# The order of the weight slots in a gated linear recurrent unit: the first y slot goes ahead of both gate slots

## The chip, the cores and the metric

The kernel runs on one core of one Trainium2 chip. The metric is the device time of one execution, in microseconds. The core's engines work at once and are ordered only by semaphores: TensorE multiplies matrices, ScalarE, VectorE and GpSimd work on elements, and SyncE issues most transfers.

## What is computed

The program is two transformer blocks over 256 tokens of width 1024: a retention mixer, a feed-forward layer, a recurrent unit (RG-LRU), a second feed-forward layer, and then a second block with an RWKV mixer, neighbourhood attention and a PEER layer. The change touches the recurrent unit alone, some 142 us of the 2104:

```
proj = x @ w_in
y_branch, u = jnp.split(proj, 2, axis=-1)          # 1536 columns each
y_branch = jax.nn.gelu(y_branch, approximate=True)
u = causal_conv4(u) + conv_b
gates = sigmoid(blockwise(u) @ gate_w + gate_b)    # 6 blocks of 256, two gates: r, i
log_a = -8 * r * softplus(-a_param)
a = exp(log_a);  b = sqrt(-expm1(2 * log_a)) * (i * u)
h[t] = a[t] * h[t-1] + b[t]                        # along the 256 tokens
return (h * y_branch) @ w_out
```

## The kernel before

**Products.** A float32 product is made of three products in a shorter type: each operand is split in a high part (a copy by ScalarE) and a low part (the difference, by VectorE), and `mm3` multiplies hi·hi, lo·hi and hi·lo.

**Slots.** All weights stream through two buffers of `SLOT` = 4096 elements per partition (2 MB; a gate slot fills 3072 of them). The list of slots is fixed; slot s uses buffer s % 2. For each slot four engines work in turn: SyncE loads it as soon as the low parts of slot s - 2 are made (`s_wlo`); ScalarE's `split_hi` (L1094, its copies are L1104) makes four pieces of the high part, once the slot is there and TensorE has drained slot s - 2 (`s_wused`); VectorE's `split_lo` (L1585) makes four pieces of the low part behind them; TensorE's `weights` (L2371) waits for the last of these.

**The recurrent unit.** Its eight slots are three u, two gate and three y slots, in the order of `LRU_STEPS`; behind them come three slots of `lru_out`, whose products add up over all twelve blocks. `LRU_STEPS` sets the order of SyncE's loads and of TensorE's work. ScalarE's and VectorE's orders are written out by hand, call by call, and must name the slots in the same order. Here a unit n is one pair of 128-wide blocks, n = 0 to 5:

- `padded(n)` (ScalarE) takes the product of a half u slot out of its bank; `convolved(n)` (VectorE, six instructions at L1806) makes the convolution; `input_hi(n)` and `input_lo(n)` split it.
- Gate products of pair n (TensorE, `gate_products`, 24 matmuls) need `input_lo(n)` and two of four banks; pair n uses banks (2n) % 4 and (2n+1) % 4, so pair 2 must wait until `sigmoids(0)` (ScalarE) has emptied those of pair 0, and so on. A gate slot holds three pairs.
- `decays(n..n+2)` (ScalarE: six exponentials L1241, six tanh L1247), `input_scale(n)` (VectorE, three instructions from L1828), `roots` (ScalarE, L1254), GpSimd's product of i and u (L1065), `scanned(n)` (VectorE, L1837 and two scans L1839).
- `gelus(n)` (ScalarE, L1260) takes y slot n out of its two banks; `gated(n)` (VectorE, L1847) multiplies h by it; `hidden_hi(n)`, `hidden_lo(n)` split the product, which slot n // 2 of `lru_out` needs.

The recurrence buffers are four (`LRU_BUFFERS`): `sigmoids(4)` waits for `gated(0)`, `sigmoids(5)` for `gated(1)`. Sigmoid, exponential (with tanh), square root and gelu each need a table of their own in ScalarE, so that a change from one to another costs an ACT_TABLE_LOAD; copies work with any table. The work behind the unit, from the last slot of `lru_out` on, is one chain: squares, `post_norm`, `norm(3)`, transposes, and the second feed-forward layer.

Of the kernel before, what the change touches and what calls it, by code (L numbers as in the profile page):

```python
# [174 lines left out]
SLOTS = {}  # L175
# [3 lines left out]
    SLOTS[_name] = sum(n for _, n in SLOTS.values()), _n  # L179
SLOTS = {k: v[0] for k, v in SLOTS.items()}  # L180

LRU_STEPS = [("u", 0), ("u", 1), ("u", 2), ("gate", 0), ("y", 0), ("gate", 1), ("y", 1), ("y", 2)]
LRU_UNITS = {"u": 2, "y": 2, "gate": 0}
LRU_SIZE = {"u": SLOT, "y": SLOT, "gate": 3072}
LRU_BUFFERS = 4
# [283 lines left out]
def first_and_second_block(nc, A, consts, out, mods, upto=99):  # L469
    cols = lambda name: consts[:, CONST_AT[name][0]:sum(CONST_AT[name])]  # L470
    with ExitStack() as ctx:
# [619 lines left out]
        def _(act):  # L1091
# [126 lines left out]
            def split_step(kind, n):  # L1218
                split_hi(lru_slot(kind, n), **lru_size(kind, n))
# [36 lines left out]
            def gelus(n):  # L1256

                for half in range(2):
                    b = take(lru_unit("y", n, half))
                    nc.scalar.activation(Y[:, 4 * n + 2 * half:4 * n + 2 * half + 2, :],  # L1260
                                         PS[:, b, :].rearrange("p (b t) -> p b t", b=2),
                                         ACT.Gelu_apprx_tanh).then_inc(s_free[b], 1)

            def padded(n):

                i, half = n // 2, n % 2
                b = take(lru_unit("u", i, half))
                if n >= 2:
                    act.wait_ge(s_uc, n - 1)
                src = PS[:, b, :].rearrange("p (b t) -> p b t", b=2)  # L1270
                nc.scalar.activation(UP[:, 2 * half:2 * half + 2, 3:3 + S], src, ACT.Copy)
                for q in range(2):
                    c = 2 * n + q
                    ins = nc.scalar.activation(UC[:, c, :], PS[:, b, half_of(q)], ACT.Identity,
                                               scale=pcol[:, PCW + 36 + c:PCW + 37 + c], bias=pcol[:, PCB + c:PCB + c + 1])
                ins.then_inc(s_free[b], 1)

            def input_hi(n):

                act.wait_ge(s_uc, n + 1)  # L1280
                nc.scalar.activation(UH[:, 2 * n:2 * n + 2, :], UC[:, 2 * n:2 * n + 2, :], ACT.Copy).then_inc(s_uhi, 1)
# [15 lines left out]
            padded(2)  # L1297
            input_hi(2)
            padded(3)
            split_step("gate", 0)  # L1300
            input_hi(3)
            padded(4)
            input_hi(4)
            padded(5)
            split_step("y", 0)
            sigmoids(0)
            input_hi(5)
            sigmoids(1)
            sigmoids(2)
            split_step("gate", 1)  # L1310
            decays(range(3))
            split_step("y", 1)
            roots(range(3))
            gelus(0)
            for n in range(3, 6):
                sigmoids(n)
            split_step("y", 2)
            hidden_hi(0)
            hidden_hi(1)
            decays(range(3, 6))  # L1320
            split_hi(SLOTS["lru_out"])
            roots(range(3, 6))
            gelus(1)
            hidden_hi(2)
# [245 lines left out]
        def _(dve):  # L1570
# [222 lines left out]
            def split_step(kind, n):  # L1793
                split_lo(lru_slot(kind, n), **lru_size(kind, n))
# [63 lines left out]
            input_lo(1)  # L1858
            convolved(2)
            input_lo(2)  # L1860
            split_step("gate", 0)
            convolved(3)
            input_lo(3)
            convolved(4)
            input_lo(4)
            split_step("y", 0)
            convolved(5)
            input_lo(5)
            split_step("gate", 1)
            for n in range(3):  # L1870
                input_scale(n)
            split_step("y", 1)
            for n in range(3):
                scanned(n)
            gated(0)
            gated(1)
            split_step("y", 2)
            hidden_lo(0)
            hidden_lo(1)
            for n in range(3, 6):  # L1880
                input_scale(n)
            split_lo(SLOTS["lru_out"])
            scanned(3)
            gated(2)
            gated(3)
# [1109 lines left out]
```

## Time and profile before

| | |
|---|---|
| median of 3 runs | 2109.35 us (2107.25 to 2112.37) |
| the profiled execution | 2105.89 us, of which the traced span is 2104.1 us |
| mean granted TensorE clock in it | 0.972 |
| TensorE busy | 1926.8 us (92%) |
| VectorE busy | 1413.4 us (67%) |
| ScalarE busy | 1041.1 us (49%) |

The busy shares are means over stages with different limits. The times in the rows below are microseconds from the span's start; the recurrent unit's products run from 469.6 to 577 us, and those of `lru_out` from 577.7 to 611.4 us.

### The profile page before, as it was taken

Reading aid. Unit: us, or ns where it says so; the run is one execution under the profiler, and the core shown is the slowest. Engines: PE = TensorE matmul, PEld = TensorE weight load, DVE = VectorE, ACT = ScalarE, POOL = GpSimd, SP = SyncE. Lnnn points to the kernel's source line nnn. Section 1 sums busy time; section 2 is a strip of 40 time slices with the busy share of each in tenths; the row PEclk is TensorE's granted clock in tenths of the full one; section 3 lists DMA queues with packets and bytes.
Section 4 is the critical chain, followed back from the end, with each engine's and each line's share of the span. In section 5 each row is a group of like instructions: output and inputs, shape, how many; then the busy total and the mean of one; then the engine's idle time right before and its main releaser. Section 6 shows DMA issues by size and latency. Waiting matters only on the chain.

```text
span 2104.1 us, 40562 instructions
## 1 busy us (share of the span) xinstructions
PE 1926.8 (92%) x15311; PEld 1723.1 (82%) x15311; DVE 1413.4 (67%) x2268; ACT 1041.1 (49%) x2078; POOL 391.4 (19%) x330
## 2 busy tenths in 40 slices
PE   6998899978889999998888769999999999999996
PEld 6875788868879888997767669999999997777775
DVE  5545587777766667325544558998899986666665
ACT  4343443445855444333444334545777765555554
POOL 2202000000100000000000003888666760000000
PEclk9999999999999999999999979999999999999998
DMA  7452556664364785413001554565544446655663
GB/s 272 170 191 90 196 186 227 234 219 139 140 220 156 249 298 201 148 71 59 2 3 43 126 122 111 165 181 152 150 141 141 140 133 189 190 189 189 189 189 130
DMA packets 212577, 333.56 MB, mean 159 GB/s; under 512 B 23494, under 2 KB 140860, under 8 KB 212424
## 3 DMA queue, kind: packets, MB, share of 16 engines
q1 hardware_dynamic: 208888, 320.06, 48.0%
q0 software_dynamic: 3536, 11.34, 1.6%
q8 instruction: 111, 1.82, 0.4%
q14 instruction: 42, 0.34, 0.1%
HBM read 330.26 MB, written 1.08 MB: 157 GB/s over the span
## 4 chain that ended last, share of the span: by engine, by line
PE 70%; DVE 15%; issue 4%; ACT 4%; DMA 2%; PEld 2%; SPq 1%; PEldq 0%; DVEq 0%; POOL 0%; ACTq 0%
PE psum L2345 20%; PE psum L2347 19%; PE psum L2346 19%; PE psum L2952 3%; DVE u_turned L2247 3%; DVE weights_lo L1585 2%; PE psum L2787 1%; PE psum L2776 1%; ACT weights_hi L1104 1%; PE psum L2781 1%; PEld psum L2345 1%; PEld psum L2346 1%; PEld psum L2347 1%; DMA rows<-mods_dram 1%; DVE lru_u L1806 1%
## 5 line engine op out<-in xcount | busy, mean ns | idle before, releaser
L1585 DVE TENSOR_TENSOR weights_lo<-weights,weights_hi 128x1024 fp32r<-128x1024 f32 (+2 forms) x336 | 345.5, 1086 | 272.4 <-ACT weights_hi L1104 267.1
L2345 PE MATMUL psum<-input_hi,weights_hi 128*128 128x256 f32 x1288 | 370.9, 288 | 14.2 <-DVE input_lo L1612 5.2
L1104 ACT ACTIVATE weights_hi<-weights 128x1024 fp32r<-128x1024 f32 (+2 forms) x336 | 289.2, 931 | 177.6 <-PEq L2392 118.0
L1083 POOL TENSOR_TENSOR u_lo<-u_turned,u_hi 128x512 fp32r<-128x512 f32 x256 | 330.7, 1314 | 200.5 <-ACT u_hi L1482 200.5
L2346 PE MATMUL psum<-input_lo,weights_hi 128*128 128x256 f32 x1288 | 367.0, 285 | 0.0
L2347 PE MATMUL psum<-input_hi,weights_lo 128*128 128x256 f32 x1288 | 366.8, 285 | 0.0
L2345 PE MATMUL psum<-input_hi,u_hi 128*128 128x256 f32 x1024 | 296.8, 290 | 6.4 <-POOL u_lo L1083 5.4
L2347 PE MATMUL psum<-input_hi,u_lo 128*128 128x256 f32 x1024 | 290.9, 284 | 0.0
L2346 PE MATMUL psum<-input_lo,u_hi 128*128 128x256 f32 x1024 | 290.7, 284 | 0.0
L2345 PEld LDWEIGHTS psum<-input_hi,weights_hi 128*128 128x128 f32 x1288 | 249.7, 194 | 29.5 <-issue 27.7
L2346 PEld LDWEIGHTS psum<-input_lo,weights_hi 128*128 128x128 f32 x1288 | 249.8, 194 | 0.0
L2347 PEld LDWEIGHTS psum<-input_hi,weights_lo 128*128 128x128 f32 x1288 | 249.6, 194 | 0.0
L2345 PE MATMUL psum<-v_hi,act_hi 128*128 128x512 f32 x512 | 203.7, 398 | 0.0
L2345 PEld LDWEIGHTS psum<-input_hi,u_hi 128*128 128x128 f32 x1024 | 197.5, 193 | 7.2 <-issue 5.8
L2347 PE MATMUL psum<-v_hi,act_lo 128*128 128x512 f32 x512 | 200.2, 391 | 0.0
L2346 PE MATMUL psum<-v_lo,act_hi 128*128 128x512 f32 x512 | 199.8, 390 | 0.0
L2346 PEld LDWEIGHTS psum<-input_lo,u_hi 128*128 128x128 f32 x1024 | 197.7, 193 | 0.0
L2347 PEld LDWEIGHTS psum<-input_hi,u_lo 128*128 128x128 f32 x1024 | 197.3, 193 | 0.0
L1482 ACT ACTIVATE u_hi<-u_turned 128x512 fp32r<-128x512 f32 x256 | 146.9, 628 | 0.0
L2319 DVE TENSOR_TENSOR act_lo<-act_table,act_hi 128x256 fp32r<-128x256 f32 x128 | 54.5, 425 | 133.8 <-ACT act_hi L1557 133.8
L1557 ACT ACTIVATE act_hi<-act_table 128x256 fp32r (+1 forms) x128 | 53.5, 418 | 166.5 <-PE psum L2347 166.2
L2247 DVE STREAM_TRANSPOSE u_turned<-u_rows 128x1024 f32<-128x1024 f32 x100 | 122.9, 1231 | 10.6 <-DMA u_rows<-in_peer_u_dram 9.8
(387 smaller groups left out, 3660.9 us busy)
## 6 DMA issues: line engine op xcount, KB each, us to landing
u_rows<-in_peer_u_dram SPq DMA_DIRECT2D x400, 128.0 KB, 2.5
weights<-in_ffn_w_in_dram SPq DMA_DIRECT2D x44, 1024.0 KB, 7.3
v_rows_even<-in_peer_v_dram SPq DMA_DIRECT2D x64, 512.0 KB, 3.5
v_rows_odd<-in_peer_v_dram SPq DMA_DIRECT2D x64, 512.0 KB, 3.4
weights<-in_ret_w_in_dram SPq DMA_DIRECT2D x24, 1024.0 KB, 7.4
ada_rows_in<-in_ada_w_dram SPq DMA_DIRECT2D x24, 1024.0 KB, 5.2
weights<-in_ffn_w_out_dram SPq DMA_DIRECT2D x44, 512.0 KB, 6.5
u_rows_more<-in_peer_u_dram SPq DMA_DIRECT2D x112, 128.0 KB, 2.6
```

What stands on the lines that cost most here:

```text
L1083: nc.gpsimd.tensor_tensor(UTL[:, b, half, :], turned[:, half, :], UTH[:, b, half, :].bitcast(F32), ALU.subtract).then_inc(s_ul[b], 1)
L1104: nc.scalar.activation(whi[:, r, at_], wraw[:, r, at_], ACT.Copy).then_inc(s_whi[r], 1)
L1482: nc.scalar.activation(UTH[:, b, half, :], turned[:, half, :], ACT.Copy).then_inc(s_uh[b], 1)
L1557: nc.scalar.activation(AH[:, j % 2:j % 2 + 1, :], GT[:, bass.ds(4 * i + j, 1), :], ACT.Copy)\
L1585: ins = nc.vector.tensor_tensor(wlo[:, r, at_], wraw[:, r, at_], whi[:, r, at_].bitcast(F32), ALU.subtract)
L1806: chain.done(nc.vector.scalar_tensor_tensor(o, UP[:, 2 * half + q, tap:tap + S], pcol[:, c:c + 1], o, ALU.mult, ALU.add))
L2247: nc.vector.transpose(UT[j % 4].rearrange("p k (c e) -> p c k e", c=4), (UR, UR2)[at_ // 2][:, at_ % 2, :].rearrange("p (c k j) -> p c k j ...
L2319: nc.vector.tensor_tensor(AL[:, b:b + 1, :], GT[:, bass.ds(4 * i + j, 1), :], AH[:, b:b + 1, :].bitcast(F32), ALU.subtract).then_inc(s_as, 1)
L2345: nc.tensor.matmul(o, ah, bh, start=start, stop=False)
L2346: nc.tensor.matmul(o, ah, bl, start=False, stop=False)
L2347: return nc.tensor.matmul(o, al, bh, start=False, stop=stop)
L2952: ins = nc.tensor.matmul(PS[:, 4 + g % 4, x * P:(x + 1) * P], ONE[:, g % 2, 1, x, :], ONE[:, g % 2, 0, x, :], start=True, stop=True)
```

## The change

`LRU_STEPS` goes from u, u, u, gate, y, gate, y, y to u, u, u, y, gate, gate, y, y. SyncE and TensorE follow it by themselves. ScalarE's and VectorE's calls are put in a new order. The instructions are the same, and as many.

```diff
--- before.py
+++ after.py
@@ -179,7 +179,7 @@
     SLOTS[_name] = sum(n for _, n in SLOTS.values()), _n
 SLOTS = {k: v[0] for k, v in SLOTS.items()}
 
-LRU_STEPS = [("u", 0), ("u", 1), ("u", 2), ("gate", 0), ("y", 0), ("gate", 1), ("y", 1), ("y", 2)]
+LRU_STEPS = [("u", 0), ("u", 1), ("u", 2), ("y", 0), ("gate", 0), ("gate", 1), ("y", 1), ("y", 2)]
 LRU_UNITS = {"u": 2, "y": 2, "gate": 0}
 LRU_SIZE = {"u": SLOT, "y": SLOT, "gate": 3072}
 LRU_BUFFERS = 4
@@ -1297,28 +1297,29 @@
             padded(2)
             input_hi(2)
             padded(3)
-            split_step("gate", 0)
+            split_step("y", 0)
             input_hi(3)
             padded(4)
             input_hi(4)
+            split_step("gate", 0)
             padded(5)
-            split_step("y", 0)
+            input_hi(5)
+            split_step("gate", 1)
             sigmoids(0)
-            input_hi(5)
             sigmoids(1)
             sigmoids(2)
-            split_step("gate", 1)
+            split_step("y", 1)
+            sigmoids(3)
+            gelus(0)
+            split_step("y", 2)
             decays(range(3))
-            split_step("y", 1)
             roots(range(3))
-            gelus(0)
-            for n in range(3, 6):
+            split_hi(SLOTS["lru_out"])
+            for n in range(4, 6):
                 sigmoids(n)
-            split_step("y", 2)
             hidden_hi(0)
             hidden_hi(1)
             decays(range(3, 6))
-            split_hi(SLOTS["lru_out"])
             roots(range(3, 6))
             gelus(1)
             hidden_hi(2)
@@ -1858,28 +1859,30 @@
             input_lo(1)
             convolved(2)
             input_lo(2)
-            split_step("gate", 0)
+            split_step("y", 0)
             convolved(3)
             input_lo(3)
             convolved(4)
             input_lo(4)
-            split_step("y", 0)
+            split_step("gate", 0)
             convolved(5)
             input_lo(5)
             split_step("gate", 1)
-            for n in range(3):
-                input_scale(n)
             split_step("y", 1)
-            for n in range(3):
-                scanned(n)
+            input_scale(0)
+            split_step("y", 2)
+            input_scale(1)
+            input_scale(2)
+            scanned(0)
             gated(0)
+            scanned(1)
             gated(1)
-            split_step("y", 2)
+            scanned(2)
+            split_lo(SLOTS["lru_out"])
             hidden_lo(0)
             hidden_lo(1)
             for n in range(3, 6):
                 input_scale(n)
-            split_lo(SLOTS["lru_out"])
             scanned(3)
             gated(2)
             gated(3)
```

ScalarE, from the end of the sixth convolution on, as a difference (`weights_hi` is a slot's high part, 128x768 for a gate slot and 128x1024 for others; `lru_r` and `lru_i` from psum are the sigmoids, `lru_a` the exponentials, `lru_y` the gelus):

```order
 L1231 ACTIVATE lru_i<-psum,param_cols 128x256 x2
 L1104 ACTIVATE weights_hi<-weights 128x1024 x4
+L1231 ACTIVATE lru_r<-psum,param_cols 128x256 x2
+L1231 ACTIVATE lru_i<-psum,param_cols 128x256 x2
+L1260 ACT_TABLE_LOAD
+L1260 ACTIVATE lru_y<-psum 128x512 x2
+L1104 ACTIVATE weights_hi<-weights 128x1024 x4
+L1241 ACT_TABLE_LOAD
+L1241 ACTIVATE lru_a<-lru_r,small 128x256 x6
+L1247 ACTIVATE lru_r<-lru_r,small 128x256 x6
```

The row of L1104 at the top is the high part of the second y slot, which now stands right behind the sigmoids of the first three pairs; the fourth pair's sigmoids, the first gelus and the third y slot's high part follow, and only then the exponentials and tanh of the first three pairs.

VectorE, from the second gate slot's low part on, in the kernel before:

```order
L1585 TENSOR_TENSOR weights_lo<-weights,weights_hi 128x768 x4
L1828 TENSOR_TENSOR lru_q<-lru_a 128x512
L1829 SCALAR_TENSOR_TENSOR lru_r<-lru_q,lru_r 128x512
L1830 TENSOR_SCALAR lru_r<-lru_r 128x512
L1828 TENSOR_TENSOR lru_q<-lru_a 128x512
L1829 SCALAR_TENSOR_TENSOR lru_r<-lru_q,lru_r 128x512
L1830 TENSOR_SCALAR lru_r<-lru_r 128x512
```

and in the kernel of the change (each line number is one higher):

```order
L1586 TENSOR_TENSOR weights_lo<-weights,weights_hi 128x768 x4
L1586 TENSOR_TENSOR weights_lo<-weights,weights_hi 128x1024 x4
L1829 TENSOR_TENSOR lru_q<-lru_a 128x512
L1830 SCALAR_TENSOR_TENSOR lru_r<-lru_q,lru_r 128x512
L1831 TENSOR_SCALAR lru_r<-lru_r 128x512
L1586 TENSOR_TENSOR weights_lo<-weights,weights_hi 128x1024 x4
L1829 TENSOR_TENSOR lru_q<-lru_a 128x512
L1830 SCALAR_TENSOR_TENSOR lru_r<-lru_q,lru_r 128x512
```

The second y slot's low part moved ahead of `input_scale(0)`, and the third y slot's low part stands between `input_scale(0)` and `input_scale(1)`.

## Rows read from the trace of the kernel before

**Rows 1.** Chain of waits, 469 to 590 us: share of the stretch by engine and line.
```profile
by line: DVE weights_lo L1585 20.9%; DVE lru_u L1806 12.8%; issue 10.2%; ACT weights_hi L1104 7.7%; ACT lru_a L1241 4.1%; ACT lru_u L1274 3.9%; DVE lru_r L1839 3.6%; DVE lru_r L1829 3.5%; PE psum L2345 3.4%; DVE lru_i L1837 3.3%; DVE lru_q 
```

**Rows 2.** Timeline, TensorE: start us, duration us, operation, [idle before it <- releaser].
```profile
505.69 0.36 PE L2345 MATMUL psum<-lru_hi,weights_hi 128*128 128x256 f32 x1 [0.37 <-issue]
...
519.60 0.55 PE L2345 MATMUL psum<-lru_hi,weights_hi 128*128 128x256 f32 x1 [7.93 <-ACT lru_r L1231]
...
547.76 0.55 PE L2345 MATMUL psum<-lru_hi,weights_hi 128*128 128x256 f32 x1 [5.35 <-ACT lru_r L1231]
...
577.74 0.47 PE L2345 MATMUL psum<-weights_hi,lru_hi 128*128 128x512 f32 x1 [0.50 <-issue]
...
589.29 0.50 PE L2345 MATMUL psum<-weights_hi,lru_hi 128*128 128x512 f32 x1 [0.40 <-DVE weights_lo L1585]
```

**Rows 3.** Timeline, VectorE, 503 to 590 us.
```profile
503.08 3.08 DVE L1806 SCALAR_TENSOR_TENSOR lru_u<-lru_padded,param_cols,lru_u 128x256 f32<-128x256 f32 x6
...
519.05 3.99 DVE L1806 SCALAR_TENSOR_TENSOR lru_u<-lru_padded,param_cols,lru_u 128x256 f32<-128x256 f32 x6
...
534.27 0.69 DVE L1828 TENSOR_TENSOR lru_q<-lru_a 128x512 f32<-128x512 f32 x1 [2.79 <-ACT lru_r L1247]
...
539.65 4.63 DVE L1585 TENSOR_TENSOR weights_lo<-weights,weights_hi 128x1024 fp32r<-128x1024 f32 x4
...
544.91 1.27 DVE L1839 TENSOR_TENSOR_SCAN lru_r<-lru_a,lru_i 128x256 f32<-128x256 f32 x2
...
551.24 1.42 DVE L1847 TENSOR_TENSOR lru_u<-lru_r,lru_y 128x512 f32<-128x512 f32 x2
...
556.05 4.81 DVE L1585 TENSOR_TENSOR weights_lo<-weights,weights_hi 128x1024 fp32r<-128x1024 f32 x4 [3.39 <-ACT weights_hi L1104]
...
564.48 0.69 DVE L1828 TENSOR_TENSOR lru_q<-lru_a 128x512 f32<-128x512 f32 x1 [2.42 <-ACT lru_r L1247]
...
584.61 4.63 DVE L1585 TENSOR_TENSOR weights_lo<-weights,weights_hi 128x1024 fp32r<-128x1024 f32 x4
```

**Rows 4.** Timeline, ScalarE, 498 to 560 us.
```profile
498.72 3.05 ACT L1104 ACTIVATE weights_hi<-weights 128x768 fp32r<-128x768 f32 x4
...
512.04 0.58 ACT L1271 ACTIVATE lru_padded<-psum 128x512 f32<-128x512 f32 x1
...
513.41 3.89 ACT L1104 ACTIVATE weights_hi<-weights 128x1024 fp32r<-128x1024 f32 x4
...
517.33 1.28 ACT L1231 ACT_TABLE_LOAD   x1
...
518.62 0.84 ACT L1231 ACTIVATE lru_r<-psum,param_cols 128x256 f32<-128x256 f32 x2
...
530.93 2.51 ACT L1241 ACTIVATE lru_a<-lru_r,small 128x256 f32<-128x256 f32 x6
...
544.38 1.08 ACT L1260 ACTIVATE lru_y<-psum 128x512 f32<-128x512 f32 x2
...
558.63 1.20 ACT L1286 ACTIVATE lru_hi<-lru_u 128x512 fp32r<-128x512 f32 x2
```

**Rows 5.** Timeline, GpSimd, 520 us.
```profile
520.27 1.44 POOL L1065 TENSOR_TENSOR lru_i<-lru_i,lru_u 128x512 f32<-128x512 f32 x1 [53.29 <-ACT lru_i L1231]
```

**Rows 6.** Weight slots, 468 to 600 us: DMA issue to landing.
```profile
DMA to landing us min/median/max: 4.5/6.7/9.3
```

**Rows 7.** Windows: window, length, busy time, then PEclk, DMA share, GB/s.
```profile
519.60:524.20 4.60, 4.43 (x24) 4.23 (x24) 3.70 (x6) 1.66 (x5) 1.44 (x1) 0.67 0.82 285
547.70:553.40 5.70, 5.46 (x24) 5.20 (x24) 4.82 (x6) 2.08 (x6) 1.66 (x1) 0.51 0.61 249
```

**Rows 8.** Timeline, TensorE, later in the program.
```profile
1181.63 0.79 PE L2345 MATMUL psum<-weights_hi,input_hi 128*128 128x512 f32 x1 [6.16 <-DVE weights_lo L1585]
...
1349.12 0.56 PE L2345 MATMUL psum<-input_hi,u_hi 128*128 128x256 f32 x1 [2.54 <-POOL u_lo L1083]
...
1431.82 0.36 PE L2345 MATMUL psum<-input_hi,u_hi 128*128 128x256 f32 x1 [2.90 <-POOL u_lo L1083]
```

## Prediction, made before the changed kernel was run

> **What bounds the kernel now.** I read the chain of waits of the recurrent unit first. Its largest shares are VectorE's low parts (20.9%), the convolutions (12.8%) and ScalarE's high parts (7.7%); TensorE's largest line has 3.4% [rows 1]. So in this stage the end is set by ScalarE and VectorE, not by TensorE. TensorE's own timeline says the same: it stands still for 7.93 us in the first gate slot and for 5.35 us in the second, both times until ScalarE's sigmoids empty a bank, and runs slow behind each [rows 2]. What decides the stage, however, is where the two sides meet. The first slot of the output product starts at 577.74, its second at 589.29, 0.40 us after TensorE had nothing left, and the releaser is the low part of that slot's weights [rows 2]. VectorE makes it from 584.61 to 589.24 [rows 3]. TensorE's finish (588.9) and VectorE's finish (589.24) are thus equal within half a microsecond. What makes TensorE earlier gives nothing, and what makes VectorE later costs in full: behind this slot comes one serial chain of products, norm and transposes with no slack to eat a delay.
>
> So I follow VectorE's program. Counted back from 589.24 it has two waits for ScalarE, 3.39 us at 556.05 and 2.42 us at 564.48, and before them one of 2.79 us, ended at 534.27 by the first tanh [rows 3]. From `input_scale(0)` at 534.27 to the low part of the second output slot at 589.24 are 55.0 us. I call the start of `input_scale(0)` S, and ask of the change: when is S, and how long is the tail behind it.
>
> **Up to the gates.** The first y slot takes the first gate slot's place. Its high parts take 3.89 instead of 3.05 us [rows 4]; its low parts take 4.63, and those of a gate slot three quarters of that, 3.5, so the convolutions behind are 1.1 us late. The y slot's low parts are there at 498.7 + 1.1 + 4.6 = 504.4, and TensorE begins it at 505.69 as it now begins the gate slot [rows 2]. The transfers have 6.7 us, at most 9.3, from issue to landing, and each slot's issue comes over 12 us before its high part; I cost the moved loads at nothing [rows 6]. TensorE does 48 matmuls in 511.67 - 505.69 = 6.0 us [rows 2], so the y slot's 96 end at 517.7. Gate 0's high part now stands ahead of `padded(5)`. That one began at 512.04 and took 1.4 [rows 4]; the high part begins at 512.04 + 1.2 = 513.2, its low part ends at 513.2 + 0.9 + 3.5 = 517.6, just in time. `padded(5)` ends at 513.2 + 3.05 + 1.4 = 517.7 and the sixth convolution at 520.8. That is 2.2 us earlier than before (523.04), 0.9 of it because no GpSimd product runs beside it: the same six instructions take 3.08 us alone and 3.99 us beside GpSimd's at 520.27 [rows 3, 5].
>
> **From there to S**, all on ScalarE. `input_hi(5)` 0.6 gives 521.4; gate 1's high part 3.05, 524.5; table load 1.28, 525.8; sigmoids are 0.73 a gate (0.84 for the two less their overlap) [rows 4]. The first bank is free at 526.6. TensorE did its 48 gate matmuls from 517.8 to 523.8, so it waits 2.8 us instead of 7.93. Here a first unknown: pair 2's 24 matmuls take 2.9 us at full clock, and took 4.43 us at 0.67 and 5.46 us at 0.51 granted after the two waits of now [rows 7]. Later in the program one wait of 2.54 us was followed by a slow matmul (0.56 us for the first) and one of 2.90 by a fast one (0.36) [rows 8]. So I keep both: pair 2 ends at 529.5 or 531.1, its sigmoids at 530.5 or 532.0. Then the second y slot's high part 3.9 (534.4 or 535.9), `sigmoids(3)` 1.5 (535.9 or 537.4), table load and two gelus 2.4 (538.3 or 539.8) [rows 4]. The third y slot's high part must wait until TensorE has drained gate 1, three pairs or 9.0 us and 0.4 after pair 2: 538.9 or 540.5. It ends at 542.8 or 544.4. The table load, the six exponentials and two tanh take from 529.6 to 534.27 now, 4.6 us [rows 3, 4]. **S = 547.4 or 549.0**, 13.1 or 14.7 us later than now. VectorE has little to do meanwhile: 5.7 us idle ahead of the second y slot's low part, then some 11 us ahead of S. The reason is that ScalarE makes two whole high parts, a pair of sigmoids and the gelus, 12.3 us with the wait, before the exponentials.
>
> The Trainium skill prices a change of table higher ("ScalarE: Activation LUTs", section "What ACT_TABLE_LOAD costs": 1.28 us for the load and about 1.38 us of draining, 2.66 in all). The row shows the load at 1.28 and the sigmoid 1.29 us after its start, so here no drain of that size is seen [rows 4]. One more load (that of gelu) stands ahead of S than before, so by the page S would be 1.4 us later still and the sum below 6.8, still inside the forecast's own case; I go by the row.
>
> **The tail behind S.** An `input_scale` is (539.65 - 534.27)/3 = 1.8; a slot's low part 4.5; a `scanned` 2.0 (0.7 and two scans); a `gated` 0.7; a `hidden_lo` 0.6, like ScalarE's `hidden_hi` of the same shape [rows 3, 4]. In VectorE's new order: scale 0, third y's low part, scale 1 and 2: 9.9. Three scans, two gated, output slot 0's low part, two `hidden_lo`: 13.2, and 0.9 for GpSimd's two products beside them [rows 5]: S + 24.0. On ScalarE from S + 9.9: a root 0.6 (taken like a gelu), output slot 0's high part 3.9, table 1.3, four gates' sigmoids 2.9, two `hidden_hi` 1.2, table 1.3, exponentials and two tanh 3.3: S + 24.4, which decides. Scale 3 to 5: S + 29.8. `gated(2)` waits for root, table and gelu, 2.4: S + 32.2. Two gated, scan, two `hidden_lo`, scan, two gated, output slot 1's low part: 12.7: **S + 44.9**. The tail is 10.1 us shorter than now's 55.0, since the second y slot's low part (4.5) now lies ahead of S and the waits of 3.39 and 2.42 are gone. The low part is therefore ready at 592.3 or 593.9 in place of 589.24: **3.1 or 4.7 us late**.
>
> **TensorE meanwhile.** Gate 1 waits for no bank; y1 ends near 551 or 552.5. The third y slot's low part stands behind `input_scale(0)` and ends at S + 6.3, 553.7 or 555.3, so TensorE waits 3 us. Output slot 0 needs `hidden_lo(1)`, S + 24.0, and lasts 588.9 - 577.7 = 11.2 [rows 2]: it is done at 582.6 or 584.2, and TensorE then waits 9.7 us for slot 1. Behind such a wait the clock is the second unknown. From rows at both levels 24 matmuls lost 1.5 (4.43 - 2.9) or 2.6 (5.46 - 2.9) or nothing; I take **1.5** [rows 7], since each wait shown of over 5 us (7.93, 5.35 and 6.16) has a slow first matmul behind it, 0.55 us at 256 columns where 0.36 is the full-speed value, 0.79 at 512 columns against 0.47 to 0.50 [rows 2, 8]. The Trainium skill ("TensorE: Matmul & The Clock Gate", section "Why this matters for your kernels") advises against idle gaps between bursts, because the clock then falls; by that rule the restart is slow for certain, which is the forecast's case and the third rival's below.
>
> **Sum.** 3.1 + 1.5 = 4.6, or 4.7 + 1.5 = 6.2; the middle, **5.4 us slower**. The profiled execution took 2105.89 us (span 2104.1), so the same with the change would take 2111.3 (span 2109.5). It lies 3.5 us under the median 2109.35, which is what I forecast from: 2114.8 us. Bounds: both clocks full, 3.1, hence 2112.4; both slow for their longest (5.46 for pair 2 adds 1.0 to S), 5.7 + 2.6 = 8.3, hence 2117.7. The runs of before spread by 2.1 below and 3.0 above their median.
>
> **Rivals.** A difference under 0.2%, 4.2 us, can't be told from none in a measurement of this kernel.
> - *The clock stays up.* Both restarts run at full speed, as after the 2.90 us [rows 8]: +3.1, 2112.4, within 0.2%. Against it: the same place is slow now after both waits. 0.26.
> - *TensorE's gain arrives.* Its waits shrink by 5.1 and 5.35, and 1.5 and 2.6 of slow clock go with them. If VectorE followed, this would arrive. It decides at S: the tail of 44.9 breaks even at S = 544.3, 0.2% is gained at S = 540.1 (2105.1), and the earliest S there is, with the exponentials right behind the third pair's sigmoids (530.5 + 4.6), would give 9.2, 2100.2. For it: S rests on the wait for TensorE's drain of gate 1 and on two copies in front of the exponentials. Against it: the rows leave 3.1 us between S and break-even even at full clock. 0.07.
> - *Both slow and long*, 2117.7: 0.13.
> - The forecast itself, between 4.2 and 7: 0.54.
>
> Together: faster 0.07, same 0.29, slower 0.64. The range is 2109.0 to 2120.0: from the first rival less the scatter of a median to the third plus it.
>
> **What would show it.** Right: VectorE idle for some 11 us, ended by tanh, at about 548; TensorE idle 2.8 (first gate slot) and none in the second, about 3 ahead of the last y slot, about 5 ahead of the output product and 9 to 10 within it; output slot 1 starting near 593. Wrong: `input_scale(0)` before 545; output slot 1 released by TensorE itself; or a stage behind the unit that is shorter than before.

## The result and the profile after

The change made the kernel slower: 2120.19 us (2117.82 to 2122.79, six runs) against 2110.43 us of the kernel before (2105.01 to 2112.95, six runs), a ratio of 1.0048 with an interval of 1.0034 to 1.0062. The forecast was 5.4 us slower, 2114.8 us, within a range that ends at 2120.0, counted from a median of before of 2109.35 us; the medians of six lie 9.8 us apart. The profiled execution took 2120.69 us, with a span of 2118.9 us at a mean granted clock of 0.967.

The same timeline of TensorE as in [rows 2], in the kernel after (start, duration, instruction, idle time before it and what ended it): first gate slot, its third pair, third y slot, output slot 0, output slot 1, and the transposes behind the norm.

```profile
518.08 0.36 PE L2348 MATMUL psum<-lru_hi,weights_hi 128*128 128x256 f32 x1 [0.52 <-DVE weights_lo L1586]
...
527.06 0.55 PE L2348 MATMUL psum<-lru_hi,weights_hi 128*128 128x256 f32 x1 [3.00 <-ACT lru_r L1231]
...
557.06 0.58 PE L2348 MATMUL psum<-input_hi,weights_hi 128*128 128x256 f32 x1 [3.17 <-DVE weights_lo L1586]
...
576.31 0.77 PE L2348 MATMUL psum<-weights_hi,lru_hi 128*128 128x512 f32 x1 [5.98 <-DVE lru_lo L1822]
...
596.96 0.80 PE L2348 MATMUL psum<-weights_hi,lru_hi 128*128 128x512 f32 x1 [7.33 <-DVE weights_lo L1586]
...
626.97 1.33 PE L2410 MATMUL psum<-ident,normed 128*128 128x128 f32 x5 [5.87 <-DVE normed L1621]
```

The change does what it says: the wait of 7.93 us in the first gate slot has become 3.00, and the one of 5.35 us in the second is gone [rows 2]. But output slot 1 starts at 596.96 in place of 589.29, behind a wait of 7.33 us for VectorE where there were 0.40, and its first matmul takes 0.80 us where it took 0.50.

VectorE's timeline, answering to [rows 3]: the second y slot's low part, `input_scale(0)` and the third y slot's low part behind it, output slot 0's low part, the second batch of scales, `gated(2)`, and output slot 1's low part.

```profile
534.38 4.88 DVE L1586 TENSOR_TENSOR weights_lo<-weights,weights_hi 128x1024 fp32r<-128x1024 f32 x4 [8.22 <-ACT weights_hi L1104]
550.59 0.69 DVE L1829 TENSOR_TENSOR lru_q<-lru_a 128x512 f32<-128x512 f32 x1 [11.33 <-ACT lru_r L1247]
...
552.39 4.62 DVE L1586 TENSOR_TENSOR weights_lo<-weights,weights_hi 128x1024 fp32r<-128x1024 f32 x4
...
568.05 6.80 DVE L1586 TENSOR_TENSOR weights_lo<-weights,weights_hi 128x1024 fp32r<-128x1024 f32 x4
...
575.98 0.68 DVE L1829 TENSOR_TENSOR lru_q<-lru_a 128x512 f32<-128x512 f32 x1
...
584.10 1.42 DVE L1848 TENSOR_TENSOR lru_u<-lru_r,lru_y 128x512 f32<-128x512 f32 x2 [0.77 <-ACT lru_y L1260]
...
592.27 4.63 DVE L1586 TENSOR_TENSOR weights_lo<-weights,weights_hi 128x1024 fp32r<-128x1024 f32 x4
```

S, the start of `input_scale(0)`, is 550.59; the tail from there to the end of output slot 1's low part is 592.27 + 4.63 - 550.59 = 46.3 us. VectorE stands idle for 11.33 us ahead of S. ScalarE's timeline, answering to [rows 4], shows what it does in that time: the third pair's two sigmoids, second y slot's high part, third y slot's high part behind a wait for TensorE's sequencer, then the table and the exponentials.

```profile
530.00 0.84 ACT L1231 ACTIVATE lru_r<-psum,param_cols 128x256 f32<-128x256 f32 x2 [0.89 <-PE psum L2350]
532.56 0.84 ACT L1231 ACTIVATE lru_i<-psum,param_cols 128x256 f32<-128x256 f32 x2 [1.72 <-PE psum L2350]
533.29 3.90 ACT L1104 ACTIVATE weights_hi<-weights 128x1024 fp32r<-128x1024 f32 x4
...
542.03 3.90 ACT L1104 ACTIVATE weights_hi<-weights 128x1024 fp32r<-128x1024 f32 x4 [0.98 <-PEq L2395]
545.95 1.28 ACT L1241 ACT_TABLE_LOAD   x1
547.24 2.52 ACT L1241 ACTIVATE lru_a<-lru_r,small 128x256 f32<-128x256 f32 x6
```

The windows of TensorE's restarts, answering to [rows 7]: third pair, third y slot, output slots 0 and 1, and the stretch behind the last (busy times are those of PE, PEld, DVE, ACT, POOL, where PE stands for TensorE's matmuls and PEld for its weight loads; then the granted clock).

```profile
527.00:533.00 6.00, 5.58 (x25) 5.34 (x25) 0.00 (x0) 3.39 (x10) 2.56 (x2) 0.50 0.97 333
557.00:560.50 3.50, 3.44 (x16) 3.44 (x17) 3.36 (x7) 0.63 (x1) 0.00 (x0) 0.51 0.70 194
576.30:580.70 4.40, 4.39 (x10) 3.45 (x11) 4.23 (x8) 2.88 (x4) 0.00 (x0) 0.50 0.90 369
596.90:601.40 4.50, 4.44 (x11) 3.48 (x12) 4.50 (x6) 0.00 (x0) 0.00 (x0) 0.50 0.71 224
601.50:607.00 5.50, 5.50 (x26) 4.54 (x25) 1.15 (x2) 0.00 (x0) 0.00 (x0) 1.00 1.08 355
```

Behind each of the four waits (3.00, 3.17, 5.98, 7.33 us) TensorE runs at half speed, 1.2 GHz, for 3.4 to 6.2 us, and then at 2.4 GHz.

**Where the time went.** The unit's first matmul starts at 469.56 in the trace of before and at 469.80 in that of after, the transposes at 617.26 and 626.97. So the stage from that matmul to the transposes has grown from 147.70 to 157.17, by 9.5 us: output slot 1 starts 7.4 us later in it, and the way from there to the transposes takes 30.0 in place of 28.0 us. That is the distance between the medians (9.8) within their scatter. The two spans lie further apart, 14.8 us, because the profiled execution of before was a fast one (2105.89, where the six have a median of 2110.43 and a lowest of 2105.01), and because other stages differ too: 1.4 us of it is a slow stretch at 632.36, behind the transposes, that the trace of before has not.

### The profile page after: what moved, and what is told of

It reads as the page before. It is cut to its first block, busy times and chain, and to the rows that moved or that the text cites. A ratio compares the mean times of both kernels' runs of the same rounds, so it can differ in the third digit from the quotient of the medians.

```text
span 2118.9 us, 40562 instructions
## 1 busy us (share of the span) xinstructions
PE 1938.2 (91%) x15311; PEld 1732.9 (82%) x15311; DVE 1414.1 (67%) x2268; ACT 1041.6 (49%) x2078; POOL 391.5 (18%) x330
## 4 chain that ended last, share of the span: by engine, by line
PE 70%; DVE 15%; issue 4%; ACT 4%; PEld 3%; DMA 2%; SPq 1%; PEldq 1%; POOL 0%; DVEq 0%; ACTq 0%
PE psum L2348 20%; PE psum L2349 19%; PE psum L2350 19%; PE psum L2955 3%; DVE u_turned L2250 2%; DVE weights_lo L1586 2%; PEld psum L2348 1%; ACT weights_hi L1104 1%; PEld psum L2349 1%; PEld psum L2350 1%; PE psum L2790 1%; PE psum L2779 1%; PE psum L2784 1%; DMA rows<-mods_dram 1%; DVE lru_u L1807 1%
## 5 line engine op out<-in xcount | busy, mean ns | idle before, releaser
L1104 ACT ACTIVATE weights_hi<-weights 128x1024 fp32r<-128x1024 f32 (+2 forms) x336 | 289.1, 930 | 180.8 <-PEq L2395 118.8
```

The source lines that it names most:

```text
L1104: nc.scalar.activation(whi[:, r, at_], wraw[:, r, at_], ACT.Copy).then_inc(s_whi[r], 1)
```

## The experiments

Each run is read at the same places. All times of this table count from the unit's first matmul, so what happens ahead of the unit is out of them. "Tail" is from S to the end of output slot 1's low part, "wait" TensorE's idle time ahead of slot 1, "end" the start of the transposes.

| kernel | S | tail | slot 1 starts | wait | slot 1 to end | end | median, us | ratio to before, 95% |
|---|---|---|---|---|---|---|---|---|
| before | 64.7 | 55.0 | 119.7 | 0.40 | 28.0 | 147.7 | 2110.43 | |
| after | 80.8 | 46.3 | 127.2 | 7.33 | 30.0 | 157.2 | 2120.19 | 1.0048 (1.0034 to 1.0062) |
| e1_low_first | 79.5 | 41.8 | 121.4 | 7.74 | 29.6 | 151.0 | 2113.12 | 1.0020 (1.0009 to 1.0031) |
| e2_decays_first | 74.8 | 47.1 | 122.0 | 8.03 | 29.3 | 151.3 | 2112.52 | 1.0029 (1.0016 to 1.0042) |
| e3_no_products | 79.6 | 45.4 | 125.1 | 8.48 | 29.5 | 154.6 | 2116.85 | 1.0047 (1.0031 to 1.0063) |
| e4_exchange | 68.5 | 54.9 | 123.5 | 1.89 | 27.9 | 151.3 | 2112.30 | 1.0019 (1.0008 to 1.0030) |
| e5_filler | 79.7 | 46.3 | 126.0 | 1.46 | 28.0 | 154.0 | 2113.22 | 1.0019 (1.0009 to 1.0028) |
| e6_filler_both | 78.2 | 46.4 | 124.7 | 0.99 | 28.0 | 152.6 | 2111.94 | 1.0023 (1.0010 to 1.0035) |
| e7_new_slots_tuned | 67.8 | 38.5 | 108.5 | 0 | 28.2 | 136.7 | 2100.46 | 0.9957 (0.9944 to 0.9971) |
| e8_old_slots_tuned | 55.6 | 43.4 | 103.2 | 0 | 28.3 | 131.5 | 2091.66 | 0.9907 (0.9889 to 0.9926) |
| e9_front | 55.6 | 56.2 | 111.9 | 2.13 | 28.0 | 139.9 | 2100.20 | 0.9955 (0.9941 to 0.9968) |
| e10_back | 64.7 | 43.3 | 112.2 | 0 | 28.3 | 140.5 | 2098.57 | 0.9940 (0.9925 to 0.9954) |
| e11_three | 78.2 | 41.8 | 120.1 | 0.31 | 27.9 | 148.0 | 2109.54 | 0.9999 (0.9990 to 1.0009) |

Each group of runs had its own runs of the kernel before: medians 2108.62 for e1 to e4, 2109.14 for e5 to e8, 2110.37 for e9 to e11. In e7, e8 and e10 the low part of slot 1 is ready before TensorE is, so "tail" is not what sets slot 1 there.

**e1: the third y slot's low part ahead of `input_scale(0)`.** VectorE's order alone:

```diff
             split_step("y", 1)
-            input_scale(0)
             split_step("y", 2)
+            input_scale(0)
             input_scale(1)
```

> The changed kernel with one call moved on VectorE: the third y slot's low part ahead of input_scale(0). Theory (VectorE's chain, S plus tail, sets the start of output slot 1): S stays at 550.6, the low part falls into VectorE's 11.3 us of idle time, the tail is one low part (4.55) shorter, output slot 1 starts at 592.4 in place of 596.96, and the time is 4 to 5 us under the changed kernel's, some 0.25% over the kernel before. Rival (TensorE's own waits and slow stretches are what the slot order costs): the 3.17 us wait ahead of the last y slot goes with its slow stretch, but output slot 1 starts no earlier than 596, and the time moves by under 1 us.

VectorE's idle time ahead of S went from 11.33 to 2.84 us, the low part of 4.63 now standing in it:

```profile
541.77 4.63 DVE L1586 TENSOR_TENSOR weights_lo<-weights,weights_hi 128x1024 fp32r<-128x1024 f32 x4 [3.73 <-ACT weights_hi L1104]
...
549.24 0.69 DVE L1829 TENSOR_TENSOR lru_q<-lru_a 128x512 f32<-128x512 f32 x1 [2.84 <-ACT lru_r L1247]
```

The tail is 41.8 in place of 46.3, shorter by one low part (4.5), and TensorE no longer waits for the third y slot. Slot 1 starts 5.8 us earlier; the other 1.3 are S, which was expected to stay and is treated under e6. VectorE's work behind S thus counts in full, and idle time ahead of S is worth nothing until something is put into it.

**e2: the exponentials ahead of the third y slot's high part.** ScalarE's order alone:

```diff
+            decays(range(3))
             split_step("y", 2)
-            decays(range(3))
             roots(range(3))
```

> The changed kernel with one call moved on ScalarE: the exponentials and tanh of pairs 0 to 2 ahead of the third y slot's high part. Theory (a late S, made by what stands ahead of the exponentials): S is at 545.7, 4.9 us earlier; but VectorE then waits for the high part behind input_scale(0) and ends the low part at 553.0 instead of 556.9, so output slot 1 starts 3.9 us earlier, at 593.1, and the time falls by about 4. Rival (S does not matter, the number of VectorE's operations does): output slot 1 at 597, no change of time.

S is 6.0 us earlier and slot 1 starts 5.2 us earlier, since the tail is 0.8 longer: VectorE now waits 0.67 us for the third y slot's high part. Of the 6.0, 4.7 are the moved copy (S was 79.5 in e1, whose third gate pair ran slow for as long as e2's); the other 1.3 are the same difference as in e1. So the third y slot's high part in front of the exponentials did hold S, as expected (4.9); the second y slot's, the other copy ahead of them, was not moved. An earlier S moves the end nearly one to one, as the rival "TensorE's gain arrives" said it would if only S were early.

**e3: GpSimd's products of pairs 4 and 5 cut to one column of 256 in each block.**

```diff
+                if n >= 4:
+                    nc.gpsimd.tensor_tensor(li[:, :, 0:1], li[:, :, 0:1], UC[:, 2 * n:2 * n + 2, 0:1],
+                                            ALU.mult).then_inc(s_liu, 1)
+                    continue
```

> The changed kernel with GpSimd's two products i times u of pairs 4 and 5 cut to one column of each block (the other columns keep i without u, so the output differs). Theory (VectorE's low part of output slot 0 takes 6.80 us in place of 4.6 because these two products run beside it): it takes 4.6 to 4.7, output slot 1 starts 2.1 us earlier, at 594.9, time 2 us under the changed kernel. Rival (it is long for another reason, as ScalarE's sigmoids beside it): it stays at 6.8 and nothing moves.

In the kernel after, the two products stand inside the output slot's low part at 568.05 (GpSimd's timeline):

```profile
568.01 1.29 POOL L1065 TENSOR_TENSOR lru_i<-lru_i,lru_u 128x512 f32<-128x512 f32 x1 [27.59 <-ACT lru_i L1231]
569.47 2.03 POOL L1065 TENSOR_TENSOR lru_i<-lru_i,lru_u 128x512 f32<-128x512 f32 x1 [0.17 <-ACT lru_i L1231]
```

Without them (VectorE's timeline of e3) the same low part takes 4.64 in place of 6.80 us, but the scales behind it then wait for ScalarE's tanh:

```profile
569.07 4.64 DVE L1590 TENSOR_TENSOR weights_lo<-weights,weights_hi 128x1024 fp32r<-128x1024 f32 x4
...
576.10 0.69 DVE L1833 TENSOR_TENSOR lru_q<-lru_a 128x512 f32<-128x512 f32 x1 [1.19 <-ACT lru_r L1251]
```

The products cost VectorE 2.2 us where I had put 0.9; of these, 0.9 reach the end (tail 46.3 to 45.4), since ScalarE's chain is due at S + 24.5 as forecast (24.4). Slot 1 starts 2.1 us earlier, the number that was expected, but by luck: 1.2 of it are S, which the products don't touch.

**e4: the exchange alone.** The kernel before with the first y slot and the first gate slot exchanged in `LRU_STEPS` and in both written orders, everything else as it was:

```diff
-LRU_STEPS = [("u", 0), ("u", 1), ("u", 2), ("gate", 0), ("y", 0), ("gate", 1), ("y", 1), ("y", 2)]
+LRU_STEPS = [("u", 0), ("u", 1), ("u", 2), ("y", 0), ("gate", 0), ("gate", 1), ("y", 1), ("y", 2)]
```

> The kernel before with only the first gate slot and the first y slot exchanged, in the slot list and in both hand-written orders; all other calls stand as in the kernel before. Theory (the cost of the change is the new place of ScalarE's and VectorE's calls, not the slot order): S is at 536 to 537 and the tail near its 55 us, output slot 1 starts at 591 to 592.5, 2 to 3 us later than in the kernel before, ratio 1.001; TensorE waits about 1, 5.6 and 7 us in the gate slots. Rival (the slot order itself costs, by TensorE's waits and clock): ratio 1.004 to 1.006 as for the changed kernel, output slot 1 past 595.

S is 3.8 us later, the tail the same within 0.1, the end 3.6 us later, the median 3.7; expected were 2 to 3. On ScalarE's timeline one sees why S moves: the first sigmoids, which before came behind gate products long done, now wait for them.

```profile
518.85 1.28 ACT L1231 ACT_TABLE_LOAD   x1
522.79 0.84 ACT L1231 ACTIVATE lru_r<-psum,param_cols 128x256 f32<-128x256 f32 x2 [2.66 <-PE psum L2347]
524.99 0.84 ACT L1231 ACTIVATE lru_i<-psum,param_cols 128x256 f32<-128x256 f32 x2 [1.36 <-PE psum L2347]
```

A part of these waits is TensorE's clock, which fell 0.6 us behind the start of these products (a wait of 1.86 us stood ahead of them); how much of the 3.8 us that is, no run separates. Windows of e4, ahead of the fall and behind it:

```profile
520.40:520.90 0.50, 0.50 (x5) 0.50 (x6) 0.46 (x2) 0.00 (x0) 0.00 (x0) 1.00 0.00 0
521.00:524.30 3.30, 3.30 (x18) 3.30 (x17) 2.09 (x5) 0.84 (x2) 0.00 (x0) 0.50 0.85 266
```

TensorE still waits long for ScalarE, 7.57 us in the second gate slot:

```profile
552.18 0.55 PE L2345 MATMUL psum<-lru_hi,weights_hi 128*128 128x256 f32 x1 [7.57 <-ACT lru_r L1231]
```

So of the 9.5 us, the exchange gives 3.6 and the reordered calls the other 5.9, as far as one profile of each kernel can tell.

**e5 and e6: TensorE kept busy.** e5 adds 56 matmuls without a use, into a bank that is free, ahead of output slot 1; e6 has these and 22 more ahead of the third gate pair.

```diff
+            def filler(b, count):
+                for _ in range(count):
+                    nc.tensor.matmul(PS[:, b, 0:S], HH[:, 0, 0:P], HH[:, 1, :], start=True, stop=True)
...
+                    if name == "lru_out" and j == 1:
+                        evacuated(lru_unit("y", 1, 0))
+                        filler(unit(lru_unit("y", 1, 0))[0], 56)
...
+                if n == 2:
+                    filler(free_bank(lru_unit("y", 1, 0)), 22)
```

> The changed kernel with 56 matmuls of 256 columns without use, into a free bank, issued by TensorE between output slots 0 and 1, where it stands still for 7.33 us. Theory (the idle wait lets the clock fall, and the slow stretch behind it costs 2.0 us): output slot 1 starts where it did, 127.2 us behind the unit's first matmul, or up to 0.3 later, without slow matmuls, and the transposes behind the product start 28.0 us after it instead of 30.0; time 2 us under the changed kernel. Rival (the slow stretch has nothing to do with the wait): it stays, and the time does not move.

> As e5_filler, and 22 such matmuls more in the 3.00 us wait ahead of pair 2's gate products. Theory: these 24 products run at full clock (2.9 us in place of 5.1 in the changed kernel's trace), the sigmoids of pair 2 end 2.2 us earlier, the third y slot's high part can start that much earlier, and S falls from 80.8 us behind the unit's first matmul to 78.3 to 79; output slot 1 follows by 2 us. Both fillers together bring 4 us against the changed kernel. Rival (S is not set by TensorE's pair 2 but by ScalarE's own sum): S stays above 80 and only the 2 us of e5 remain.

TensorE in e5, the last seven matmuls of the filler and then slot 1 behind a wait of 1.46 us, with a matmul of 0.40 us where the kernel after had 0.63:

```profile
594.28 1.00 PE L2431 MATMUL psum<-input_hi 128*128 128x256 f32 x7
596.74 0.50 PE L2348 MATMUL psum<-weights_hi,lru_hi 128*128 128x512 f32 x1 [1.46 <-DVE weights_lo L1586]
597.07 0.40 PE L2349 MATMUL psum<-weights_lo,lru_hi 128*128 128x512 f32 x1
```

From slot 1 to the end now 28.0 us, as before the change, in place of 30.0. The slow restart behind the wait for slot 1 costs 2.0 us in the kernel after, then, and that it is the clock is shown. In e1, e2 and e3, which have the same restart without a filler, it cost 1.6, 1.3 and 1.5 us. In e6 the third gate pair runs at full clock too, its first window here (the second is the fourth pair's):

```profile
528.00:531.40 3.40, 3.10 (x24) 2.90 (x24) 0.00 (x0) 3.08 (x9) 2.52 (x2) 1.00 0.90 282
531.50:534.00 2.50, 2.50 (x21) 2.50 (x22) 1.04 (x1) 2.50 (x5) 1.30 (x1) 1.00 1.05 397
```

and S is 78.2, earlier than in any run with the change's ScalarE order but e11's, which has the same filler and the same S. Without it S was 80.8 in the kernel after and 79.5 to 79.7 in e1, e3 and e5, though all four wait the same 2.98 to 3.00 us ahead of that pair. What differs is how long TensorE stays slow: e1 for 2.7 us, 12 matmuls; the kernel after for 6.2 us, 25 matmuls, the whole pair. In e1, the restart and what follows:

```profile
526.90:529.80 2.90, 2.85 (x13) 2.88 (x14) 0.00 (x0) 2.09 (x6) 2.00 (x2) 0.50 0.79 261
529.90:533.00 3.10, 2.73 (x23) 2.56 (x23) 0.00 (x0) 2.48 (x5) 1.19 (x2) 1.00 1.05 398
```

So pair 2's slow clock costs S 1.3 to 2.6 us, and which of the two one profile shows is not decided by the order of instructions: up to that pair e5 is the kernel after, instruction by instruction. (The 5.1 us that e6's expectation gives for the slow pair are 5.5 in the trace.) The medians of e5 and e6, 4.1 and 2.8 us above that of before, lie lower than the ends of their stages would have them (+6.3 and +4.9); those come from one profile each, the difference was not followed. By the ratios of the table, 4.0 and 4.9 us, the times do not tell e5 and e6 apart, so what the second filler brings rests on the profiles alone.

**e11: e1 and both fillers.**

> The changed kernel with e1's move of the third y slot's low part and both fillers of e6 together. Theory (the three terms add: S with its slow pair, the tail, the slow restart): S at 78.2, the tail 41.8, output slot 1 at 120.0, nothing slow behind it, transposes at 148.0 behind the unit's first matmul against 147.7 in the kernel before: the whole loss is accounted for, ratio 0.999 to 1.001. Rival (a part of the loss lies elsewhere, in the later stages): transposes at 148 but ratio above 1.002.

The stage ends 0.3 us behind that of the kernel before, and the ratio is 0.9999. The three repairs add up: 157.2 - 4.5 (low part) - 2.6 (S) - 2.1 (restart) = 148.0, which is what was measured. Mending these three places takes back the whole of what the change costs, in the stage and in the time of the whole kernel. GpSimd's two products still run beside the low part in e11 (its tail is e1's); they are part of the change's 46.3, but that tail is shorter than before's 55.0 even so.

**e7 and e8: orders looked for anew.** Both have the same kind of calls in another order, worked out from the durations of the rows; e7 for the new list of slots, e8 for the old one. e8's order, ScalarE and then VectorE, where it differs most from the kernel before:

```diff
-            split_step("gate", 0)
-            input_hi(3)
             padded(4)
-            input_hi(4)
-            padded(5)
+            split_step("gate", 0)
             split_step("y", 0)
             sigmoids(0)
-            input_hi(5)
+            padded(5)
             sigmoids(1)
-            sigmoids(2)
+            input_hi(3)
+            input_hi(4)
             split_step("gate", 1)
-            decays(range(3))
+            sigmoids(2)
+            decays(range(0, 3))
+            input_hi(5)
...
             hidden_lo(0)
+            scanned(2)
+            input_scale(3)
+            input_scale(4)
+            split_lo(SLOTS["lru_out"] + 0)
             hidden_lo(1)
-            for n in range(3, 6):
-                input_scale(n)
-            split_lo(SLOTS["lru_out"])
-            scanned(3)
             gated(2)
+            input_scale(5)
+            split_lo(SLOTS["lru_out"] + 1)
+            scanned(3)
             gated(3)
```

> The changed slot list with another order of ScalarE's and VectorE's calls: high and low parts earlier than the elementwise work that does not feed them, the next pair's convolution begun while the last one's input is split, first gelus ahead of the first sigmoids, exponentials ahead of the third y slot's high part, output slot 1's parts ahead of the last scans. Theory (VectorE's chain is what costs, and the slot list leaves room): output slot 1 starts 107 to 110 us behind the unit's first matmul instead of 119.7 in the kernel before and 127.2 in the changed one, ratio 0.994 to 0.996. Rival (the new slot list costs in itself, by TensorE): no faster than the kernel before.

> The kernel before's slot list with an order of calls made in the same way: the first sigmoids as soon as the first gate products are there, ahead of the fifth and sixth pair. Theory (the order of calls decides, not the slot list): output slot 1 starts 104 to 107 us behind the unit's first matmul, TensorE's waits of 7.93 and 5.35 us shrink to under 1, ratio 0.992 to 0.994, a little faster than the new list with its order. Rival (the new list with its paired gate slots is the better one once the order fits): e7_new_slots_tuned is faster than this.

e7 came out within its expectation, e8 a little below: slot 1 at 103.2 where 104 to 107 were expected. e8 is the fastest kernel of the study, 2091.66 us, 0.9907 of the kernel before (0.9889 to 0.9926); its stage is 16.2 us shorter. Its TensorE has no wait of over 1.1 us from the first gate slot to the end of the output product, and no slow stretch, and its S is 9.1 us earlier:

```profile
529.15 0.36 PE L2349 MATMUL psum<-lru_hi,weights_hi 128*128 128x256 f32 x1 [0.37 <-issue]
...
535.37 0.36 PE L2349 MATMUL psum<-lru_hi,weights_hi 128*128 128x256 f32 x1 [0.23 <-ACT lru_r L1231]
...
539.55 0.39 PE L2349 MATMUL psum<-input_hi,weights_hi 128*128 128x256 f32 x1 [1.08 <-DVE weights_lo L1586]
...
563.83 0.47 PE L2349 MATMUL psum<-weights_hi,lru_hi 128*128 128x512 f32 x1 [0.50 <-DVE lru_lo L1822]
```

e7, with the new list, is 11.1 us shorter than the kernel before and 20.5 than the kernel after. So the calls are worth more than the list, and with the best order that I found for each, the old list is ahead by 5.2 us in the stage; whether a better order for the new list closes that is not shown.

**e9 and e10: the halves of e8.** e9 has e8's order up to the exponentials and `input_scale(2)`, and the old one behind; e10 the reverse: sigmoids in two groups, output slots 1 and 2 split earlier.

> The kernel before with only the front of e8_old_slots_tuned's order: ScalarE's calls up to the first exponentials, VectorE's up to input_scale(2); the rest in the old order. Theory (S and the tail add up): S falls from 64.7 to 55.6 behind the unit's first matmul, the tail stays near 55 with a longer wait in it, since the pair products of the second gate slot still wait behind the first gelus; output slot 1 starts at 111 to 113 instead of 119.7, ratio 0.996. Rival (only the tail's order matters): no change.

> The other half alone: the old order up to the first exponentials, e8_old_slots_tuned's from there on. Theory: S stays at 64.7, the tail falls by 8, to where TensorE itself decides (output slot 1 released by nothing), output slot 1 starts at 111 to 112.5, ratio 0.996. Rival (only an earlier S matters): no change.

The stage is shorter by 7.8 us in e9 and by 7.2 in e10, together 15.0 of e8's 16.2; slot 1 starts at 111.9 and 112.2, both as expected. In e9 S is 9.1 earlier and slot 1 only 7.8, with TensorE waiting 2.13 us for its low part: what the front gains, VectorE's old order behind it gives back in part. In e10 S is where it was, and slot 1's low part, made at 572.93 in place of 584.61, is there before TensorE asks for it. The medians fell by more (10.2 and 11.8 us), again by differences outside the unit.

## Why the prediction was wrong, and where it was right

The sign, the mechanism and the place were right; the size was not. The measured 2120.19 us lie 0.2 above the range's end. That end allowed for 10.65 us over 2109.35, and 9.8 were measured over 2110.43, so it is the higher median of before that puts the time outside; but the forecast's own bound of 8.3 us was passed in any case. TensorE's waits fell as forecast (2.8 forecast and 3.00 measured in the first gate slot, none in the second, 3 and 3.17 ahead of the last y slot, 5 and 5.98 ahead of the output product), the kernel grew slower all the same, VectorE idled 11.33 us (forecast 11) up to a tanh, and output slot 1 is released by VectorE. One of the signs missed: TensorE waits 7.33 us for slot 1 and not "9 to 10 within it", because slot 0, too, ran partly at half speed and took 13.3 us where 11.2 were put; that costs nothing, as slot 1 waits for VectorE. What failed is the size: 5.4 forecast, 9.5 in the stage. Three terms of the sum were too small.

- **S.** "S = 547.4 or 549.0"; measured 550.59, and 550.35 without the 0.24 us by which the whole unit started later. The step that failed is "pair 2 ends at 529.5 or 531.1". I priced a slow pair at 4.43 us, the row at a granted clock of 0.67 [rows 7], and kept the row at 0.51 (5.46) for the bounds. The pair ran slow from end to end and took some 5.5. Against the middle of my two values, 548.2, S was 2.1 us later. Over more runs the middle is nearer: e6 and e11 put the value for full clock at 78.2 from the unit's start, 547.8 on the axis of before (forecast 547.4), and three runs at 79.5 to 79.7, 549.1 to 549.2 (forecast 549.0). As values both branches were right, but weighing them alike was not: in all five profiles with the wait of 3.0 us (after, e1, e2, e3, e5) the pair ran slow, in four of them in 4.4 to 4.5 us, and only a filler gave full clock. So of the 2.1 us, 0.8 is the half weight on full clock, and the rest, 1.3, mostly the longer stretch that the profile of after drew and that only my bounds held.
- **The tail.** "S + 44.9"; measured 46.3, so 1.4 more. "0.9 for GpSimd's two products" was taken from a convolution, six instructions of 128x256, next to one product [rows 5]. Two products beside a slot's low part cost 2.2. As ScalarE's S + 24.4 had 0.4 us of room over VectorE's S + 24.0, 1.0 of the missing 1.3 reached the end; e3 confirms it from the other side with 0.9. The other 0.4 us lie in the serial part behind.
- **The restart.** "I take 1.5"; against e5 it is 2.0 in the kernel after, between the two rows I had. With 1.3 to 1.6 in e1 to e3, 1.5 was a fair value, and the missing 0.5 is one profile's draw.

Together 2.1 + 1.4 + 0.5 = 4.0 on top of 5.4 give 9.4, against 9.5 measured. My upper bound, both restarts at their longest, gave 8.3; it held GpSimd's share at 0.9, so the bound stopped short although the clock did no more than it allowed for (5.5 us for pair 2, 2.0 for the restart). The tail is thus the one term that failed whatever the clock did. A bound should take in every term that was priced from an unlike row.

The rival "the clock stays up" would have been 3.1 slower. Its test is e6, where both restarts run at full speed: the stage is 4.9 us longer than before's, 1.8 above the rival's 3.1, of which some 1.4 are the tail and 0.4 S. e11 shows that with both restarts at full speed, and with VectorE's idle time used as well, the change comes out at no difference. The rival "TensorE's gain arrives" needed S at 544.3; e2 had it at 74.8 from the unit's start, 544.4 on the axis of before, but still ended 3.6 us later: 2.2 by its tail of 47.1 (0.7 of that the wait for the third y slot's high part) and 1.3 by its slow restart. The break-even of 544.3 was thus too late: it had a tail of 44.9 and no restart in it.

As for the table switch: the load takes 1.28 us and the exponential starts 1.29 us after it (545.95 and 547.24 in the rows above), as in the kernel before. The Trainium skill ("ScalarE: Activation LUTs", section "What ACT_TABLE_LOAD costs") adds 1.38 us of draining; the trace doesn't agree here either, and that its sum of 6.8 was nearer to 9.5 is by a term that wasn't there. The Trainium skill's rule against idle gaps ("TensorE: Matmul & The Clock Gate", section "Why this matters for your kernels") is borne out at all four waits of the kernel after, and in e5 and e6 by taking gaps away. It does not hold without exception: in e5 a wait of 3.17 us ahead of the third y slot was followed by full speed (granted 1.00 from 556.9 to 560.5).

## What to carry to other kernels

A wait that is removed from an engine is worth something only if that engine's work is awaited last; here TensorE's 13.3 us of waits in the gate slots fell to 3.0 and the stage grew by 9.5, because the longer chain hung on ScalarE's exponentials, and these had been put behind more copies. Find the place at which the two chains meet (here output slot 1, 0.40 us of slack), and move work from behind the longer chain's last wait into the idle time ahead of that wait; the one low part moved in e1 gave its full 4.5 us. And where two engines' orders are written by hand, look for a better order of the calls before changing the order of the data: with the slots as they were, the calls alone gave 17.5 us, 16.2 of them in this stage.

## What the runs showed of the chip that I had not expected

- The same wait of 2.98 to 3.00 us at the same place was followed by slow stretches of 2.7 (e1, e2), 2.9 (e3), 3.1 (e5) and 6.2 us (the kernel after). A single profile of such a place is one draw.
- The length of a wait alone did not tell what followed. The wait of 3.17 to 3.18 us ahead of the third y slot was followed by half speed for 3.4 us (the kernel after) and 6.1 us (e6), by a late fall (e3, below) and by full speed (e5). Of the shorter ones, 2.13 us (e9), 1.89 (e4) and 1.46 (e5) ahead of output slot 1 were followed by full speed, but 1.86 (e4, first gate slot), 2.16 and 1.74 (e7, second gate slot and third y slot) by a fall of the granted clock to 0.50 within 1.3 us. And the 1.7 us behind the transposes, ahead of the second feed-forward layer, were followed by a slow first matmul (0.55 us) in ten of the thirteen profiles and by a fast one (0.36) in those of before, e6 and e8.
- The fall need not come at the restart. In e3, behind a wait of 3.18 us, TensorE began at full speed and fell after eleven matmuls, in the midst of unbroken work (the last three lines stand one behind the other):

```profile
558.08 0.39 PE L2352 MATMUL psum<-input_hi,weights_hi 128*128 128x256 f32 x1 [3.18 <-DVE weights_lo L1590]
...
559.37 0.28 PE L2353 MATMUL psum<-input_lo,weights_hi 128*128 128x256 f32 x1
559.49 0.36 PE L2354 MATMUL psum<-input_hi,weights_lo 128*128 128x256 f32 x1
559.65 0.42 PE L2352 MATMUL psum<-input_hi,weights_hi 128*128 128x256 f32 x1
```

- Two products of GpSimd (128x512, 1.29 and 2.03 us) stretched four instructions of VectorE (128x1024) from 4.64 to 6.80 us: VectorE lost 2.2 us to 3.3 us of GpSimd's work, and the second product took 0.7 us more than the first. Without the products (e3) the four instructions took 4.64 us.
